# Attention group C: three pairs of score banks, one bank for transposed blocks and one for values

## The chip, the cores and the metric

One core of a Trainium2 chip runs the whole program. The metric is device time in microseconds (us). TensorE (PE) does the matmuls and the transposes, VectorE (DVE) and ScalarE (ACT) work on tiles, GpSimd (POOL) helps them, and SyncE (SP) issues the DMAs. PE writes to PSUM, a memory of 8 banks of 512 float32 per partition. Each engine executes its own list of instructions in order; a wait on a semaphore holds up everything behind it in that list.

## The reference, cut to what matters

The model has two layers. Each has three attention groups over 1024 positions, an output projection and a gated MLP. The change concerns group C, differential attention: four heads, each with two softmax maps over keys of width 32 and a distance bias; the second map is subtracted from the first with a learned weight, and the difference multiplies the values.

```python
logits = jnp.einsum('bqhid,bshid->bhiqs', qb, k).astype(f32) * scale
bias = -slopes[:, None, None, None] * jnp.abs(qp[:, None] - pos[None, :])[None, None]
p = jax.nn.softmax(logits + bias, axis=-1)
a = (p[:, :, 0] - lam * p[:, :, 1]).astype(v.dtype)
return jnp.einsum('bhqs,bshe->bqhe', a, v)
```

## The kernel before, in words

A layer's attention is a row of 32 units: units 0 to 7 are group B, units 8 to 15 group C (U_C is 8), units 16 to 31 group A (U_A is 16). A unit is one head and one half of the queries (512 of them, in four tiles of 128). Its work has these parts.

- Scores (`score_item`, L1645): one item is a tile of 128 queries against all 1024 keys, two PSUM banks wide. A unit of A or B has 4 items. A unit of C has 8, two maps for each query tile.
- Maximum (`max_item`, L1250 in group C, L1253 in the others): DVE adds the distance bias to the item in PSUM and takes its row extreme in one pass.
- Exponential (`exp_item`, L925): ACT reads the item from PSUM and writes it to SBUF, and sums the rows.
- Mix (`mix_maps`, group C alone): the second map, scaled by the ratio of the row sums, is added to the first. DVE does it for three query tiles (L1316, L1317, L1322), GpSimd for the first one (L708, L710), for which DVE only computes the ratio.
- Transposes and value product: in steps s = 0 to 7 PE transposes four 128x128 blocks of the probabilities into one PSUM bank (L1717), ACT copies the bank to SBUF (L987), and in groups A and B DVE computes a low part from it as well (L1358, called ptl). Three steps later (LAG) PE multiplies the copy with the values (L1679 in group C, L1683 and L1684 in A and B), which adds up over the eight steps in one bank.
- Spread reciprocals (L1730, called the norm): DVE inverts the row sums (`reciprocal_sums`, L1331), PE transposes them with a broadcast into a bank, ACT copies that bank to `nrm` (`copy_norm`, L961).
- Output sum (`sum_output`, L1340 in group C, L1343 in the others): DVE multiplies or adds the value bank. In A and B ACT copies one half of the bank first (`copy_part`, L970). Then ACT and GpSimd split the result into a high and a low part (L975, L700).

The units are staggered. While unit x is transposed, the items of the next unit are scored, reduced and exponentiated: items 2 to 7 at steps 0 to 5 of x (`STEP_OF[6]`). At steps 6 and 7 items 0 and 1 of the unit after the next follow (`EARLY_STEP_OF`). On ACT the exponentials of items 1 to 7 stand at steps 0 to 6 (`EXP_STEP_OF[6]`), and item 0 of the unit behind at step 7; in group C each stands ahead of the copy of its step. On DVE the mixes 0 to 3 of the next unit stand at steps 1, 4, 6 and 7, the last ahead of the maximum of item 1. PE begins step 0 of a C unit only when all four mixes are done. These orders are written out by hand in `pe_unit`, `act_unit` and `dve_unit`; no planner is at work.

The eight banks: two pairs for scores (banks 0 and 1, banks 2 and 3), taken in turn, so that a score waits for the exponential two items back; banks 4 and 5 for transposed blocks in turn, so that step s waits for the copy of s-2 (`transposed_free`); banks 6 and 7 for values, by the half of the queries. The norm is written to the value bank of the other half, at step 6, when the output sum of the unit before has read it, and ACT copies it out at step 6 or, in group C, 7. The output sum of the unit before stands at step 3 on DVE, behind the maximum of that step.

## Time and profile before

| what | us |
|---|---|
| median of 3 runs (lowest, highest) | 2998.17 (2997.57, 2999.02) |
| the profiled execution, its own time | 2998.82 |
| its span, first to last instruction | 2997.0 |
| PE busy | 2899.7 (97%) |
| DVE busy | 1991.8 (66%) |
| ACT busy | 1316.1 (44%) |
| POOL busy | 457.0 (15%) |
| mean granted TensorE clock | 0.993 of full speed |

The time of a run is a little longer than the span, as it holds what lies around the first and the last instruction. Busy shares are means over the whole program. Group C is transposed from 361 to about 499 us in layer 0, and from 1834 to about 1972 us in layer 1; its scores begin two units earlier.

### The profile page before, as it was taken

To read this page: it belongs to the slowest core of one execution; us is meant where nothing else is said; L and a number is where in the kernel's file an instruction comes from. 1 tells how busy PE (TensorE), PEld (TensorE's weight loads), DVE (VectorE), ACT (ScalarE), POOL (GpSimd) and SP (SyncE) were. 2 spreads that over 40 slices of the span, in tenths; PEclk is the share of its full clock that TensorE was granted. 3 is DMA by queue.
4 is the path that set the end of the run, shared out by engine and by line. 5 is a ranking of instruction groups with operands and counts; after the bars stand their busy time and mean duration, and the time that the engine had idled before them with its cause. 6 is when DMAs were issued, how large, how long until landed. Compare 5 with 4: busy or idle time off the path is not lost.

```text
span 2997.0 us, 36868 instructions
## 1 busy us (share of the span) xinstructions
PE 2899.7 (97%) x13564; PEld 2315.2 (77%) x13564; DVE 1991.8 (66%) x2312; ACT 1316.1 (44%) x1839; POOL 457.0 (15%) x243
## 2 busy tenths in 40 slices
PE   7999889999999999999999998899999999999998
PEld 5777656888788888888877785578887888888887
DVE  3987887982465556556678778889716565556555
ACT  4326888992322222222333287889714212212223
POOL 1211332223300000000131023322341000000002
PEclk9999999999999999999999999999999999999999
DMA  5455332432112111111135633234312111111102
GB/s 195 151 169 126 83 82 61 93 91 76 43 56 60 53 42 56 42 42 42 40 132 200 171 90 71 64 85 100 104 45 68 43 43 56 42 42 56 56 28 57
DMA packets 236372, 236.48 MB, mean 79 GB/s; under 512 B 59488, under 2 KB 199520, under 8 KB 236256
## 3 DMA queue, kind: packets, MB, share of 16 engines
q1 hardware_dynamic: 236256, 234.94, 27.8%
q8 instruction: 72, 1.18, 0.2%
q14 instruction: 44, 0.36, 0.0%
HBM read 184.04 MB, written 50.86 MB: 78 GB/s over the span
## 4 chain that ended last, share of the span: by engine, by line
PE 85%; DVE 7%; issue 4%; ACT 3%; DMA 1%; SPq 0%; POOL 0%; ACTq 0%; DVEq 0%
PE ps L1795 29%; PE ps L1810 16%; PE ps L1545 16%; PE ps L1645 8%; PE ps L1717 6%; PE ps L1683 3%; PE ps L1684 3%; DVE ps L1250 2%; PE ps L1679 2%; PE ps L1780 2%; PE ps L1576 1%; PE ps L1730 1%; DVE prob L1322 1%; DVE rstd L1395 0%; DVE r L1235 0%
## 5 line engine op out<-in xcount | busy, mean ns | idle before, releaser
L1645 PE MATMUL ps<-stack 128*128 128x512 f32 (+1 forms) x1152 | 347.5, 419 | 44.1 <-ACT prob L925 19.1
L1444 DVE TENSOR_TENSOR xT<-ps,xT 128x512 f32<-128x512 f32 x352 | 241.9, 691 | 214.4 <-PE ps L1810 214.2
L1645 PEld LDWEIGHTS ps<-stack 128*128 128x128 f32 (+1 forms) x1152 | 206.7, 191 | 154.9 <-ACT prob L925 51.3
L1717 PEld LDWEIGHTS ps<-cst,prob 128*128 128x128 f32 x2048 | 254.7, 142 | 89.1 <-issue 19.9
L1717 PE MATMUL ps<-cst,prob 128*128 128x128 f32 x2048 | 310.5, 275 | 7.5 <-issue 4.0
L925 ACT ACTIVATE prob<-ps,nmx 128x1024 f32<-128x1024 f32 x256 | 284.6, 1112 | 22.8 <-PE ps L1717 12.3
L1358 DVE TENSOR_TENSOR ptl<-ps,pth 128x512 fp32r<-128x512 f32 x384 | 259.3, 685 | 47.6 <-ACT pth L987 40.9
L1409 DVE SCALAR_TENSOR_TENSOR cv<-u,vec,cv 128x1024 f32<-128x1024 f32 x176 | 225.8, 1283 | 88.0 <-ACT cv L1064 77.8
L1076 ACT ACTIVATE ah<-cv 128x1024 fp32r<-128x1024 f32 x44 | 46.7, 1061 | 533.2 <-DVE cv L1422 533.2
L1795 PE MATMUL ps<-xgh,w0h 128*128 128x512 f32 x704 | 274.0, 389 | 2.6 <-ACT sq L1056 2.6
L1795 PE MATMUL ps<-xgl,w0h 128*128 128x512 f32 x704 | 273.9, 389 | 0.0
L1795 PE MATMUL ps<-xgh,w0l 128*128 128x512 f32 x704 | 273.9, 389 | 0.0
L1253 DVE TENSOR_REDUCE nmx<-ps 128x1 f32<-128x1024 f32 x192 | 234.0, 1219 | 60.0 <-PE ps L1645 58.5
L1064 ACT ACTIVATE cv<-u,vec 128x1024 f32<-128x1024 f32 x88 | 109.6, 1246 | 354.4 <-DVE u L1403 353.8
L987 ACT ACTIVATE pth<-ps 128x512 fp32r<-128x512 f32 x384 | 229.0, 597 | 68.8 <-PE ps L1717 59.9
L1795 PE MATMUL ps<-xgh,w1h 128*128 128x512 f32 x640 | 249.8, 390 | 4.1 <-DVE u L1403 4.1
L1795 PE MATMUL ps<-xgh,w1l 128*128 128x512 f32 x640 | 249.7, 390 | 0.0
L1795 PE MATMUL ps<-xgl,w1h 128*128 128x512 f32 x640 | 249.5, 390 | 0.0
L1810 PE MATMUL ps<-ah,dnh 128*128 128x512 f32 x640 | 249.1, 389 | 0.0
L1810 PE MATMUL ps<-ah,dnl 128*128 128x512 f32 x640 | 249.0, 389 | 0.0
L1810 PE MATMUL ps<-al,dnh 128*128 128x512 f32 x640 | 249.0, 389 | 0.0
L1403 DVE TENSOR_TENSOR u<-ps,rstd 128x512 f32<-128x512 f32 x176 | 118.7, 688 | 195.1 <-PE ps L1795 195.0
(239 smaller groups left out, 5554.4 us busy)
## 6 DMA issues: line engine op xcount, KB each, us to landing
wraw<-in_w_up SPq DMA_DIRECT2D x88, 512.0 KB, 4.7
draw<-in_w_down SPq DMA_DIRECT2D x22, 1024.0 KB, 4.9
stack<-ka_d SPq DMA_DIRECT2D x64, 256.0 KB, 5.7
wraw<-in_w_in SPq DMA_DIRECT2D x30, 512.0 KB, 4.2
vst<-v_d SPq DMA_DIRECT2D x48, 256.0 KB, 3.8
x_d<-xT SPq DMA_DIRECT2D x2, 4096.0 KB, 17.6
wraw<-in_w_out SPq DMA_DIRECT2D x16, 512.0 KB, 5.4
stack<-qc_d SPq DMA_DIRECT2D x64, 128.0 KB, 3.4
```

The costliest lines, as they stand in the source:

```text
L925: act.activation(two(dst), score_banks(i), ACT.Exp, bias=nmx[:, b, i:i + 1], scale=scale, accum_out=rsum[:, b, i:i + 1]).then_inc(exp_done, 1)
L987: act.activation((ptf if x["group"] == "C" else pth)[:, s % NPT, :], ps[:, 4 + s % 2, :], ACT.Copy).then_inc(pt_hi, 1)
L1253: dve.tensor_reduce(nmx[:, b, i:i + 1], src, AX.XY, ALU.max, negate=True).then_inc(max_done, 1)
L1358: dve.tensor_tensor(ptl[:, s % NPT, :], ps[:, 4 + s % 2, :], pth[:, s % NPT, :].bitcast(F32), ALU.subtract).then_inc(pt_lo, 1)
L1403: ins = dve.tensor_tensor(u[:, c, 1 + b * HALF:1 + (b + 1) * HALF], ps[:, base + 2 * c + b, :], rstd[:, b * HALF:(b + 1) * HALF], ALU.mult)
L1409: return dve.scalar_tensor_tensor(cv[:, c, :], u[:, c, k:k + T], vec[:, bass.ds(f + (V_CONV + 2 * k * FT + c * FT), 1)], cv[:, c, :], ALU. ...
L1444: ins = dve.tensor_tensor(xs, ps[:, 4 + j % 4, :], xs, ALU.add)
L1545: ins = pe.matmul(outs[b], a, x_[:, b * HALF:(b + 1) * HALF], start=start and n == 0, stop=stop and n == 2)
L1645: ins = pe.matmul(score_banks(i)[:, kh, :], st[q][0:rows, c0:c0 + P], st[k][0:rows, kh * HALF:(kh + 1) * HALF], start=n == 0, stop=n == le ...
L1717: ins = pe.transpose(ps[:, 4 + s % 2, m * P:(m + 1) * P], prob[:, b, m, s * P:(s + 1) * P], ident)
L1795: ins = pe.matmul(ps[:, base + 2 * c + b, :], a[:, o:o + P], x_[:, k, b * HALF:(b + 1) * HALF], start=k == 0 and n == 0, stop=k == KT - 1 ...
L1810: ins = pe.matmul(ps[:, 4 + j % 4, :], a[:, f, t * P:(t + 1) * P], x_[:, slot + f, b * HALF:(b + 1) * HALF], start=n == 0, stop=n == 5)
```

## The change: what it does

In group C the scores take three pairs of banks in turn (0 and 1, 2 and 3, 4 and 5), by the table `PAIRS`. The first C unit keeps the two pairs of before; the second uses the table mirrored. Bank 6 holds all transposed blocks of group C, bank 7 all its values. The spread reciprocals take pair 1 (bank 2) between its items 3 of one unit and 0 of another, in the last C unit bank 5; they move on PE from step 6 to step 3, and their copy on ACT from step 7 to step 4. The output sum of the unit before moves on DVE ahead of the maximum of step 3, and in the first C unit ACT's copy of a half moves ahead of the exponential of step 3.

The waits follow the banks. A score of the items 2 to 5 (and of item 1 from the fourth C unit on) waits for the exponential three items back; the others wait for two back. Item 0 also waits for the copy of the spread reciprocals two units back. Item 2 of the second C unit waits for the last low part of group B. In group C step s of the transposes waits for the copy of s-1, and the first value product waits for the output sum of the unit before. Groups A and B keep their banks. The first A unit gets two more waits, on copies of the spread reciprocals.

The diff, with lines of its context left out:

```diff
--- before.py
+++ after.py
@@ -351,9 +351,32 @@
-        def score_banks(i):
-
-            return ps[:, 2 * ((i + 1) % 2):2 * ((i + 1) % 2) + 2, :]
+        PAIRS = (1, 2, 0, 1, 2, 0, 2, 0)
+        NORM_PAIR = 1
+        def score_pair(x, i):
+            c = x["k"] - U_C
+            if x["group"] != "C" or c == 0:
+                return (i + 1) % 2
+            return (2 - PAIRS[i] if c == 1 else PAIRS[i])
+        def score_banks(x, i):
+            n = 2 * score_pair(x, i)
+            return ps[:, n:n + 2, :]
+        def trans_bank(x, s):
+            return ps[:, 6 if x["group"] == "C" else 4 + s % 2, :]
+        def value_bank(x):
+            return 7 if x["group"] == "C" else 6 + x["half"]
+        def norm_bank(x):
+            if x["group"] != "C":
+                return 7 - x["half"]
+            return 5 if x["k"] == U_A - 1 else 2 * NORM_PAIR
@@ -922,7 +945,7 @@
                         dst, scale = prob[:, b, i, :], 1.0
-                    act.activation(two(dst), score_banks(i), ACT.Exp, bias=nmx[:, b, i:i + 1],
+                    act.activation(two(dst), score_banks(x, i), ACT.Exp, bias=nmx[:, b, i:i + 1],
                                    scale=scale, accum_out=rsum[:, b, i:i + 1]).then_inc(exp_done, 1)
@@ -958,7 +981,7 @@
                     act.wait_ge(o_ready, l * NU + x["u"] + O_CREDIT)
-                    act.activation(nrm[:, :], ps[:, 7 - x["half"], :], ACT.Copy).then_inc(norm_copied, 1)
+                    act.activation(nrm[:, :], ps[:, norm_bank(x), :], ACT.Copy).then_inc(norm_copied, 1)
@@ -977,6 +1000,8 @@
                         second = nx and nx["group"] == "C"
+                        if s == 3 and x["k"] == U_C:
+                            copy_part(prev)
                         item = EXP_STEP_OF[own_items(nx)].get(s) if nx else None
@@ -984,14 +1009,14 @@
                         act.wait_ge(av_done, l * (8 * NU) + x["u"] * 8 + s + 1 - NPT + AV_CREDIT)
-                        act.activation((ptf if x["group"] == "C" else pth)[:, s % NPT, :], ps[:, 4 + s % 2, :], ACT.Copy).then_inc(pt_hi, 1)
+                        act.activation((ptf if x["group"] == "C" else pth)[:, s % NPT, :], trans_bank(x, s), ACT.Copy).then_inc(pt_hi, 1)
                         if not second and item is not None:
                             exp_item(nx, item)
-                        if s == 3 and prev:
+                        if s == 3 and prev and x["k"] != U_C:
                             copy_part(prev)
...
                             hi_mix(prev)
-                        if s == (7 if x["group"] == "C" else 6):
+                        if s == (4 if x["group"] == "C" else 6):
                             copy_norm(x)
@@ -1241,7 +1266,7 @@
                     dve.wait_ge(scores_done, l * NS + x["item0"] + i + 1)
-                    src = score_banks(i)
+                    src = score_banks(x, i)
                     if x["group"] == "C":
@@ -1337,7 +1362,7 @@
                         dve.wait_ge(mix_lo, l * NU + x["u"] + MIX_CREDIT)
-                        dve.tensor_tensor(osum[rows, :], ps[rows, 6 + x["half"], :], nrm[rows, :], ALU.mult).then_inc(o_ready, 1)
+                        dve.tensor_tensor(osum[rows, :], ps[rows, value_bank(x), :], nrm[rows, :], ALU.mult).then_inc(o_ready, 1)
                         return
@@ -1347,6 +1372,8 @@
                             mix_maps(nx, MIX_STEPS[s])
+                        if s == 3 and x["group"] == "C":
+                            sum_output(prev)
                         if nx and s in STEP_OF[own_items(nx)]:
@@ -1358,7 +1385,7 @@
                             reciprocal_sums(x)
-                        if s == 3 and prev:
+                        if s == 3 and prev and x["group"] != "C":
                             sum_output(prev)
@@ -1631,7 +1658,13 @@
                         pe.wait_ge(z_ready, l * NT + NT - 1 + i)
-                    pe.wait_ge(exp_done, l * NS + it - 1 + EXP_CREDIT)
+                    c = x["k"] - U_C if x["group"] == "C" else 0
+                    far = (c >= 1 and 2 <= i <= 5) or (c >= 2 and i == 1 and c > 2)
+                    pe.wait_ge(exp_done, l * NS + it - (2 if far else 1) + EXP_CREDIT)
+                    if i == 0 and (c >= 2 or x["k"] == U_A):
+                        pe.wait_ge(norm_copied, l * NU + x["u"] - 2 + 1 + N_CREDIT)
+                    if c == 1 and i == 2:
+                        pe.wait_ge(pt_lo, l * (8 * NAB) + U_C * 8 + PT_CREDIT)
                     qt = i // 2 if x["group"] == "C" else i
@@ -1642,7 +1675,7 @@
                         for kh in range(2):
-                            ins = pe.matmul(score_banks(i)[:, kh, :], st[q][0:rows, c0:c0 + P], st[k][0:rows, kh * HALF:(kh + 1) * HALF],
+                            ins = pe.matmul(score_banks(x, i)[:, kh, :], st[q][0:rows, c0:c0 + P], st[k][0:rows, kh * HALF:(kh + 1) * HALF],
                                             start=n == 0, stop=n == len(terms) - 1)
@@ -1659,6 +1692,13 @@
+                    if x["group"] == "C":
+                        if s == 0:
+                            pe.wait_ge(norm_copied, l * NU + x["u"] + N_CREDIT)
+                        pe.wait_ge(pt_hi, l * (8 * NU) + x["u"] * 8 + s)
+                        return
+                    if x["k"] == U_A and s == 1:
+                        pe.wait_ge(norm_copied, l * NU + x["u"] + N_CREDIT)
                     y, n = (x, s - 1) if s >= 2 else (prev, s + 7)
@@ -1675,8 +1715,12 @@
                     if x["group"] == "C":
+                        if s == 0 and x["k"] == U_C:
+                            pe.wait_ge(o_read, l * NAB + x["u"] + O_CREDIT)
+                        elif s == 0:
+                            pe.wait_ge(o_ready, l * NU + x["u"] + O_CREDIT)
                         pe.wait_ge(pt_hi, l * (8 * NU) + x["u"] * 8 + s + 1)
-                        pe.matmul(ps[:, 6 + b, :], vfull[x["par"]][:, s, :], ptf[:, s % NPT, :],
+                        pe.matmul(ps[:, value_bank(x), :], vfull[x["par"]][:, s, :], ptf[:, s % NPT, :],
                                   start=s == 0, stop=s == 7).then_inc(av_done, 1)
@@ -1714,20 +1758,23 @@
                         for m in range(4):
-                            ins = pe.transpose(ps[:, 4 + s % 2, m * P:(m + 1) * P], prob[:, b, m, s * P:(s + 1) * P], ident)
+                            ins = pe.transpose(trans_bank(x, s)[:, m * P:(m + 1) * P], prob[:, b, m, s * P:(s + 1) * P], ident)
                         ins.then_inc(trans_done, 1)
...
                             value_product(prev, 8 + s - LAG)
-                        if s == 6:
+                        if s == (3 if x["group"] == "C" else 6):
                             pe.wait_ge(dinv_done, l * NU + x["u"] + 1)
-                            if prev and prev["group"] == "C":
+                            if x["group"] == "C":
+                                if nx["group"] == "C":
+                                    pe.wait_ge(exp_done, l * NS + nx["item0"] + 4 + EXP_CREDIT)
+                            elif prev and prev["group"] == "C":
                                 pe.wait_ge(o_ready, l * NU + prev["u"] + 1 + O_CREDIT)
...
                             for m in range(4):
-                                ins = pe.transpose(ps[:, 7 - b, m * P:(m + 1) * P], dinv[:, m:m + 1].to_broadcast([P, P]), ident)
+                                ins = pe.transpose(ps[:, norm_bank(x), m * P:(m + 1) * P], dinv[:, m:m + 1].to_broadcast([P, P]), ident)
                             ins.then_inc(norm_done, 1)
...
```

## Rows read from the trace of the kernel before

**Rows 1.** The page, part 1: busy us of each engine over the span.

```profile
PE 2899.7 (97%) x13564; PEld 2315.2 (77%) x13564; DVE 1991.8 (66%) x2312; ACT 1316.1 (44%) x1839; POOL 457.0 (15%) x243
```

**Rows 2.** Windows, a unit each: length, PE, PEld, DVE, ACT, POOL; clock, DMA, GB/s.

```profile
393.96:411.34 17.38, 15.57 (x68) 9.07 (x68) 15.55 (x30) 14.43 (x27) 6.48 (x3) 1.00 0.25 69
411.34:429.12 17.78, 15.80 (x69) 9.07 (x69) 15.87 (x30) 14.44 (x27) 6.48 (x3) 1.00 0.37 82
```

**Rows 3.** Timeline of DVE, one round: start, duration, instruction; idle before and releaser.

```profile
392.53 1.26 DVE L1250 CUSTOM_DVE_ANT_0 ps<-ps,dtab 128x1024 f32<-128x1024 f32 x1
...
397.13 1.22 DVE L1250 CUSTOM_DVE_ANT_0 ps<-ps,dtab 128x1024 f32<-128x1024 f32 x1
...
400.62 1.23 DVE L1250 CUSTOM_DVE_ANT_0 ps<-ps,dtab 128x1024 f32<-128x1024 f32 x1 [1.03 <-PE ps L1645]
...
402.38 1.23 DVE L1250 CUSTOM_DVE_ANT_0 ps<-ps,dtab 128x1024 f32<-128x1024 f32 x1
...
404.15 1.23 DVE L1250 CUSTOM_DVE_ANT_0 ps<-ps,dtab 128x1024 f32<-128x1024 f32 x1 [0.47 <-PE ps L1645]
...
405.30 0.68 DVE L1340 TENSOR_TENSOR osum<-ps,nrm 64x512 f32<-64x512 f32 x1
...
405.91 1.23 DVE L1250 CUSTOM_DVE_ANT_0 ps<-ps,dtab 128x1024 f32<-128x1024 f32 x1
...
409.91 1.27 DVE L1250 CUSTOM_DVE_ANT_0 ps<-ps,dtab 128x1024 f32<-128x1024 f32 x1
```

**Rows 4.** Timeline of PE in the same round: scores, transposes, value products, norm.

```profile
397.31 0.63 PE L1717 MATMUL ps<-cst,prob 128*128 128x128 f32 x4
...
399.70 0.73 PE L1645 MATMUL ps<-stack 128*128 128x512 f32 x2 [0.90 <-ACT prob1a L925]
...
400.27 0.60 PE L1717 MATMUL ps<-cst,prob 128*128 128x128 f32 x4
...
400.71 1.02 PE L1679 MATMUL ps<-ptf,vfull 128*128 128x512 f32 x2
...
401.29 0.91 PE L1645 MATMUL ps<-stack 128*128 128x512 f32 x2
...
402.03 0.60 PE L1717 MATMUL ps<-cst,prob 128*128 128x128 f32 x4
...
402.47 1.02 PE L1679 MATMUL ps<-ptf,vfull 128*128 128x512 f32 x2
...
410.42 0.60 PE L1730 MATMUL ps<-cst,dinv 128*128 128x128 f32 x4
```

**Rows 5.** Timeline of ACT in the same round: exponential of item 1, copy of step 0.

```profile
398.44 1.11 ACT L925 ACTIVATE prob1a<-ps,nmx 128x1024 f32<-128x1024 f32 x1 [0.54 <-DVE nmx L1250]
...
399.55 0.59 ACT L987 ACTIVATE ptf<-ps 128x512 f32<-128x512 f32 x1
```

**Rows 6.** Timeline of PE in unit 14, packed around the norm.

```profile
479.33 1.02 PE L1679 MATMUL ps<-ptf,vfull 128*128 128x512 f32 x2
480.19 0.60 PE L1730 MATMUL ps<-cst,dinv 128*128 128x128 f32 x4
480.55 1.18 PE L1645 MATMUL ps<-stack 128*128 128x512 f32 x4
481.57 0.60 PE L1717 MATMUL ps<-cst,prob 128*128 128x128 f32 x4
```

**Rows 7.** Timeline of DVE in units 7 and 8: ptl, maximum, output sum, a mix.

```profile
362.19 0.69 DVE L1358 TENSOR_TENSOR ptl<-ps,pth 128x512 fp32r<-128x512 f32 x1
...
362.80 1.22 DVE L1250 CUSTOM_DVE_ANT_0 ps<-ps,dtab 128x1024 f32<-128x1024 f32 x1
...
369.97 0.68 DVE L1343 TENSOR_TENSOR osum<-ps,osum 64x512 f32<-64x512 f32 x1 [0.61 <-ACT osum L970]
...
372.31 1.78 DVE L1322 SCALAR_TENSOR_TENSOR prob<-prob1a,rinv,prob 128x1024 f32<-128x1024 f32 x1
```

**Rows 8.** Window of 2 us in layer 1, unit 8, columns as in rows 2.

```profile
1838.00:1840.00 2.00, 2.00 (x7) 1.61 (x6) 1.59 (x5) 1.88 (x4) 0.25 (x1) 0.50 0.02 4
```

## The prediction

> **What bounds the kernel now.** I read the busy shares first: TensorE is busy for 97% of the span [rows 1], so most of the kernel is matmul-bound and an edit of group C can't touch it. Next I read busy time unit by unit. The change concerns group C alone, units 8 to 15 of each layer. In a C unit of 17.4 us the reader is to see PE at 15.57, DVE at 15.55 and ACT at 14.43 [rows 2]: none is full, so the unit is bound by a chain that goes round the engines. To find it I read three engines' instructions of one unit in order of time [rows 3 to 5].
>
> I call the score items of the unit after next a0 to a7, the first item behind them b0, and T(s), V(s) the transposes and the value product of step s. One round is from max a0 (DVE, 392.53) to max b0 (409.91), 17.38 us. DVE idles in it twice: 1.03 us ahead of max a3 (400.62) and 0.47 ahead of max a5 (404.15) [rows 3]. Before max a3 the chain is: the last mix, max a1 (397.13), exp a1 on ACT (398.44), and only then the score of a3 on PE (399.70, after 0.90 idle), since with two pairs a3 takes the pair that exp a1 empties [rows 3 to 5]. From there PE runs packed: a step is 1.76 (T at 400.27 and 402.03), of which T to V is 0.44, V to the next score 0.75, score to T 0.57; V to the next T is 1.32 [rows 4]. From max a6 (405.91) to max b0 DVE is packed for 4.00 us [rows 3]. N, the spread reciprocals at step 6 (410.42), stands where PE next waits for an exp anyway [rows 4], so N is free now.
>
> **Part 1, the third pair.** The scores of items 2 to 5 (and 1 from the fourth unit on) wait for an exp one further back. So score a3 can follow as soon as T(0) and V(5) are through: 397.31 + 0.44 + 0.75 = 398.50, its end at 399.24, and max a3 0.19 later (DVE follows a matmul's end by that: 399.70 + 0.73 to 400.62), 399.43 instead of 400.62 [rows 3, 4]. Taken alone this gives DVE 1.19 us.
>
> **Part 2, one transposed bank.** T(s) now waits for the copy of s-1, where it waited for s-2. In ACT's queue copy(0) stands behind exp a1, and exp a1 stands behind max a1 and DVE's mixes: copy(0) starts at 399.55 and takes 0.59, so 400.14 [rows 5]. T(1) can start at about 400.19; before it started at 400.27 [rows 4]. The score of a4 stands behind T(1) and V(6) in PE's queue. So the lead of 1.19 us ends at T(1): a4 is scored only 0.08 sooner than before, and DVE idles before a4 instead of before a3. That is what is late next.
>
> In the other steps this wait is met: beside T (0.60) ACT has an exp of 1.11, then the copy of 0.59, a ring of 1.70 against PE's own 1.76 [rows 4, 5]. The Trainium skill (Perfetto Trace Analysis, "Optimizing Tensor Performance", Matmuls) says that groups of matmuls should rotate through different PSUM banks, so that the evacuation of one overlaps the next. By that rule each of the eight transposes of a unit would pay for the single bank; the rows say that only T(1) does.
>
> **Part 3, one value bank.** V(0) of a unit now waits for the output sum of the unit before, moved on DVE ahead of max a5. V(7) of that unit starts at 402.39 (402.47 less 0.08) and ends 1.02 later, DVE follows by 0.19, the sum takes 0.68, and PE follows by about 0.1 (an estimate between 0.05 and that 0.19): 404.38 [rows 3, 4]. By PE's own pace V(0) would be at 402.39 + 1.32 + 0.44 = 404.15. Cost 0.23; bounds 0.05 (every wake-up at its shortest) and 0.68 (the whole sum exposed). I take 0.23, which is built from the nearest rows.
>
> **Part 4, N moved from step 6 to step 3.** The four transposes are the same; they stand now between V(0) and the score of a6, in the packed stretch. Where PE is packed around N, V to N is 0.86, N to the score 0.36, N to the next T 1.38 with a score of four matmuls [rows 6]; two fewer end 0.45 sooner (1.18 against 0.73). So V to T grows from 1.32 to 0.86 + 0.93 = 1.79: cost 0.47. Bounds: 0 (if it all fits under what PE waits for) and 0.86. N's wait for exp a3 is met, as T(3) has waited for copy(2), which is behind it in ACT's queue. What N leaves at step 6 gains nothing: the score there waits for exp a7, which DVE sets. Copying N out at step 4 on ACT, 0.6 us, lies in the time in which ACT waits for max a6.
>
> **The new round.** V(0) 404.38, N 405.24, score a6 ends 0.36 + 0.73 later at 406.33, max a6 at 406.52 instead of 405.91. Before, DVE itself set this point, with the sum (405.30) behind a5; moving the sum gives DVE a slack that it can't use. Then DVE's 4.00 us, b0 at 410.52. The round is 17.99, +0.61. The longer rounds of 17.78 [rows 2] pay their 0.4 more around the same sum, where it now overlaps in part: I take +0.3. Of the rounds of units 9 to 13 three are short and two long in each layer: 3 x 0.61 + 2 x 0.3 = 2.4. Unit 14 passes the same points up to its last mix: +0.6. From unit 15 on PE has no gap between its pieces (how they close up around N: [rows 6]); N only changes its place: 0.
>
> **The first C unit.** Score 2 of unit 9 takes banks 4 and 5, and so waits for the last ptl of unit 7, which starts on DVE at 362.19: end 362.88, score at 362.98, max 2 at 363.90 [rows 7]. Before, that max started right behind the ptl, at 362.80. +1.1. Later in the unit V(0) waits for ACT's copy of a half and DVE's sum (ends 370.65 before); with the same steps max 6 comes 1.6 later, of which DVE's slack gives 0.5 back. I take +1.1, between 0.7 and 1.6. PE stands for some 4 us ahead of that score. In layer 1 a stretch of this unit already shows a granted clock of 0.50 of full speed, 1.2 GHz, after several shorter stands [rows 8]; if layer 0 falls too, that is 1 us more.
>
> **Sum.** 2.4 + 0.6 + 1.1 = 4.1 a layer, 8.2 in two. The profiled execution took 2998.82 (span 2997.0), 0.65 above the median of 2998.17: from its own time the new one is 3007.0, on the median 3006.4. Forecast 3006.4, its own range 3003.5 to 3010. About 0.2%, 6 us, is what can be told from no change.
>
> **Rivals.** (A) The other side: T(1) isn't held. If copy(0) ends before 399.07, where T(1) could go behind the early score (398.50 + 0.57), the 1.19 us come through to a4; V(0)'s wait and N take 0.7 back, and the round is 16.9. That is -0.5 for three rounds and unit 14, -0.87 for two, +1.1: -2.6 a layer, 2992.9. If N and the sum were hidden as well, DVE would lose its 1.50 of idle in six stretches: 2981. Against it: exp a1 stands behind DVE's packed mixes, and copy(0) behind exp a1, a full microsecond late for it. (B) N and the sum's wait are hidden (bounds 0 and 0.05), and only the first unit costs: +2.2, 3000.4. For it: TensorE's weight loads overlap, and my rows on N come from a stretch with other scores. (C) Worse: the sum now runs beside GpSimd's mix and is stretched to its upper bound, 0.45 more in six stretches of each layer, and layer 0's clock falls: +6.4, 3012.8. For it: one mix on DVE grew from 1.28 to 1.78 while GpSimd worked [rows 7]; against it: that was another operation. (D) The pair isn't used as it says, since items 6, 7 and 0 keep the near wait: the same time as the forecast, as T(1) takes over either way.
>
> **Chances.** Forecast 0.58 (with D), A 0.13, B 0.17, C 0.12. Slower by over 0.2% (above 3004.2): 0.91 of the forecast and all of C, 0.65. Within 0.2%: the rest of the forecast, B and half of A, 0.28. Faster: the other half of A, 0.07. The range leaves out A and a little above C: 2999 to 3013.
>
> **What would show it.** Right: in a middle C unit the score of a3 comes 1.2 us sooner, while T(1) starts right behind copy(0); DVE idles ahead of max a4 and ahead of max a6, over 1 us each; PE waits some 0.2 before V(0); N is followed by its score at once; the round is near 18.0; max 2 of unit 9 comes 1.1 later. Wrong: rounds of 17.3 or less; or equal rounds, with N in a stall; or a loss outside group C.

## The result and the profile after

| | before | after |
|---|---|---|
| median of 6 runs, us (lowest, highest) | 2998.06 (2996.99, 2999.02) | 3009.72 (3006.04, 3012.50) |
| the profiled execution, us | 2998.82 | 3008.77 |
| its span, us | 2997.0 | 3007.0 |

The ratio of the times is 1.0036, 95% interval 1.0026 to 1.0046: the change makes the kernel slower, by 11.7 us on the medians and by 10.0 in the profiled pair. Forecast was 3006.4, with 2999 to 3013 as the range.

The busy shares don't tell the story. The page, part 1 of after, beside [rows 1]:

```profile
PE 2896.9 (96%) x13564; PEld 2317.5 (77%) x13564; DVE 1990.2 (66%) x2312; ACT 1315.5 (44%) x1839; POOL 457.1 (15%) x243
```

Each engine does the same work in more time, so the loss is waiting. Part 5 of the page groups it by line; the last column is idle time ahead of the group and the releaser of most of it. Before, scores and transposes:

```profile
L1645 PE MATMUL ps<-stack 128*128 128x512 f32 (+1 forms) x1152 | 347.5, 419 | 44.1 <-ACT prob L925 19.1
...
L1717 PE MATMUL ps<-cst,prob 128*128 128x128 f32 x2048 | 310.5, 275 | 7.5 <-issue 4.0
```

After, the same two lines of the code:

```profile
L1678 PE MATMUL ps<-stack 128*128 128x512 f32 (+1 forms) x1152 | 369.1, 438 | 27.3 <-ACT prob L948 12.8
...
L1761 PE MATMUL ps<-cst,prob 128*128 128x128 f32 x2048 | 312.7, 276 | 35.0 <-ACT ptf L1012 20.7
```

The idle time ahead of scores falls by 16.8 us: the part that waits for exponentials, over all three of their tiles, goes from 43.3 to 17.9, and 9.3 are new, for the last ptl of group B. Ahead of the transposes 27.5 us are added, and 20.7 of what stands there now waits for the copy out of the one bank. The wait has changed its line and grown.

Where in time: I measured every round of group C, from the maximum of one unit's item 0 to that of the next, in both profiled executions.

| round, by the unit that is transposed | before, layer 0 / 1 | after, layer 0 / 1 | change | predicted |
|---|---|---|---|---|
| unit 8 | 19.25 / 19.74 | 22.32 / 22.31 | +3.07 / +2.57 | +1.1 |
| units 9 to 13, sum | 87.68 / 87.69 | 90.40 / 90.41 | +2.72 / +2.72 | +2.4 |
| unit 14, to the maximum of item 7 | 16.22 / 16.25 | 16.97 / 16.96 | +0.75 / +0.71 | +0.6 |

Together that is +12.5 us, where 8.2 was predicted. The span grew by 10.0, so in this pair 2.5 us came back outside group C. The single times of before in the experiments below lie between 2992 and 3003, so a difference of that size needs no cause in the change. The stretches outside group C, where the code is nearly the same in every kernel of this document, say so too: together they took between 2741.9 and 2754.3 us in the twelve profiled executions, 2750.2 in before's and 2747.6 in after's.

**A middle unit.** Windows of after, beside [rows 2]: length, PE, PEld, DVE, ACT, POOL, clock, DMA share, GB/s:

```profile
398.22:416.33 18.11, 15.39 (x68) 9.25 (x68) 15.44 (x30) 14.38 (x27) 6.48 (x3) 1.00 0.23 66
416.33:434.47 18.14, 15.40 (x68) 9.26 (x68) 15.69 (x30) 14.35 (x27) 6.47 (x3) 1.00 0.37 80
```

Timeline of DVE in the round from max a0 to max b0, beside [rows 3]:

```profile
396.79 1.26 DVE L1275 CUSTOM_DVE_ANT_0 ps<-ps,dtab 128x1024 f32<-128x1024 f32 x1
...
401.39 1.23 DVE L1275 CUSTOM_DVE_ANT_0 ps<-ps,dtab 128x1024 f32<-128x1024 f32 x1
...
403.72 1.26 DVE L1275 CUSTOM_DVE_ANT_0 ps<-ps,dtab 128x1024 f32<-128x1024 f32 x1
...
406.62 1.23 DVE L1275 CUSTOM_DVE_ANT_0 ps<-ps,dtab 128x1024 f32<-128x1024 f32 x1 [1.16 <-PE ps L1678]
...
407.77 0.68 DVE L1365 TENSOR_TENSOR osum<-ps,nrm 64x512 f32<-64x512 f32 x1
408.38 1.23 DVE L1275 CUSTOM_DVE_ANT_0 ps<-ps,dtab 128x1024 f32<-128x1024 f32 x1
...
410.90 1.23 DVE L1275 CUSTOM_DVE_ANT_0 ps<-ps,dtab 128x1024 f32<-128x1024 f32 x1 [1.23 <-PE ps L1678]
...
414.90 1.27 DVE L1275 CUSTOM_DVE_ANT_0 ps<-ps,dtab 128x1024 f32<-128x1024 f32 x1
```

Take each start from the round's own beginning. Max a3 comes at 6.93, where before it came at 8.09: the third pair delivers its 1.16. Max a4 comes at 9.83, before at 9.85: the whole lead is gone one item later, as idle time of 1.16. Max a6 comes at 14.11 where it was at 13.38, with 1.23 of idle ahead of it.

PE in the same round, beside [rows 4], shows who took it:

```profile
398.71 0.66 PE L1761 MATMUL ps<-cst,prob 128*128 128x128 f32 x4 [0.83 <-ACT ptf L1012]
...
401.57 0.63 PE L1761 MATMUL ps<-cst,prob 128*128 128x128 f32 x4 [0.88 <-DVE prob L1347]
...
402.50 1.03 PE L1678 MATMUL ps<-stack 128*128 128x512 f32 x2
404.45 0.66 PE L1761 MATMUL ps<-cst,prob 128*128 128x128 f32 x4 [0.93 <-ACT ptf L1012]
...
405.41 1.02 PE L1678 MATMUL ps<-stack 128*128 128x512 f32 x2
406.27 0.60 PE L1761 MATMUL ps<-cst,prob 128*128 128x128 f32 x4
...
408.03 0.60 PE L1761 MATMUL ps<-cst,prob 128*128 128x128 f32 x4
408.70 1.10 PE L1723 MATMUL ps<-ptf,vfull 128*128 128x512 f32 x2
409.64 0.60 PE L1777 MATMUL ps<-cst,dinv 128*128 128x128 f32 x4
410.00 0.71 PE L1678 MATMUL ps<-stack 128*128 128x512 f32 x2
```

The score of a3 (402.50) no longer idles. T(1), 404.45, waits 0.93 for the copy of step 0. V(0), 408.70, starts 0.67 behind T(3) where V follows T by 0.44 elsewhere, which I read as its wait for the output sum; two rounds on, the trace names it at the same place:

```profile
445.14 1.10 PE L1723 MATMUL ps<-ptf,vfull 128*128 128x512 f32 x2 [0.27 <-DVE osum L1365]
```

N, 409.64, stands 0.94 behind V(0) in the packed stretch. The first line, 398.71, is T(7) of the unit before. It too waits for the copy of the step before it, which stands behind an exponential. That costs nothing: T(7) comes 1.92 into the round and came 2.00 into it before, and T(0), held by the last mix, comes at 4.78 in both. So of the waits for that copy on the page about half, those ahead of T(7), are idle time without a loss.

ACT, beside [rows 5], shows why the copy of step 0 is late; the first exponential is that of item a1:

```profile
402.71 1.11 ACT L948 ACTIVATE prob1a<-ps,nmx 128x1024 f32<-128x1024 f32 x1 [1.04 <-DVE nmx L1275]
...
403.81 0.59 ACT L1012 ACTIVATE ptf<-ps 128x512 f32<-128x512 f32 x1
404.29 1.11 ACT L948 ACTIVATE prob<-ps,nmx 128x1024 f32<-128x1024 f32 x1
```

T(0) is done at 402.20, but ACT, in order, first waits for max a1 (1.04 of idle) and does exp a1. The copy could have started while ACT idled.

**The first unit.** PE and then DVE of after while unit 8 is transposed, beside [rows 7]:

```profile
363.68 1.19 PE L1678 MATMUL ps<-stack 128*128 128x512 f32 x2 [4.66 <-DVE ptl L1385]
364.67 1.05 PE L1761 MATMUL ps<-cst,prob 128*128 128x128 f32 x4
...
372.24 1.10 PE L1723 MATMUL ps<-ptf,vfull 128*128 128x512 f32 x2 [0.89 <-DVE osum L1368]
...
377.98 0.71 PE L1678 MATMUL ps<-stack 128*128 128x512 f32 x2 [0.69 <-ACT prob L948]
```

```profile
365.06 1.23 DVE L1275 CUSTOM_DVE_ANT_0 ps<-ps,dtab 128x1024 f32<-128x1024 f32 x1 [1.53 <-PE ps L1678]
...
374.42 1.23 DVE L1275 CUSTOM_DVE_ANT_0 ps<-ps,dtab 128x1024 f32<-128x1024 f32 x1 [1.20 <-PE ps L1678]
```

The score of item 2 stands 4.66 us until the last ptl has read its banks, as predicted. Behind it matmuls take longer: this score 1.19 instead of 0.73, the transposes 1.05 instead of 0.60. Windows of the two layers (the clock is the third number from the end), beside [rows 8]:

```profile
361.00:365.00 4.00, 1.32 (x4) 1.05 (x5) 2.53 (x4) 1.20 (x2) 1.78 (x1) 0.55 0.00 0
365.00:369.00 4.00, 4.00 (x16) 3.26 (x15) 2.62 (x6) 2.45 (x5) 0.00 (x0) 0.60 0.00 0
```

```profile
1840.00:1844.00 4.00, 2.27 (x8) 1.91 (x9) 2.47 (x4) 1.40 (x3) 0.96 (x1) 0.50 0.00 0
1844.00:1848.00 4.00, 4.00 (x19) 3.24 (x18) 2.62 (x8) 3.22 (x5) 0.51 (x1) 0.72 0.01 2
```

The granted clock falls to 0.50 of full speed, 1.2 GHz, in both layers. Before it fell in layer 1 alone. Measured from each round's start in layer 0, max 2 comes 1.61 later than before, max 4 2.50, max 5 3.19, max 6 3.20 and the next round 3.07. ACT gives a last piece:

```profile
376.19 0.60 ACT L984 ACTIVATE nrm<-ps 128x512 f32<-128x512 f32 x1 [0.88 <-POOL osum L717]
```

The copy of N, moved to step 4, waits here for GpSimd, and the exponential of item 6 stands behind it.

### The profile page after: what moved, and what is told of

It reads as the page before. It is cut to its first block, busy times and chain, and to the rows that moved or that the text cites. A ratio compares the mean times of both kernels' runs of the same rounds, so it can differ in the third digit from the quotient of the medians.

```text
span 3007.0 us, 36900 instructions
## 1 busy us (share of the span) xinstructions
PE 2896.9 (96%) x13564; PEld 2317.5 (77%) x13564; DVE 1990.2 (66%) x2312; ACT 1315.5 (44%) x1839; POOL 457.1 (15%) x243
## 4 chain that ended last, share of the span: by engine, by line
PE 85%; DVE 7%; issue 3%; ACT 3%; DMA 1%; POOL 1%; SPq 0%; ACTq 0%; DVEq 0%; POOLq 0%
PE ps L1842 29%; PE ps L1857 16%; PE ps L1572 16%; PE ps L1678 8%; PE ps L1761 6%; PE ps L1727 3%; PE ps L1728 3%; DVE ps L1275 2%; PE ps L1723 2%; PE ps L1827 2%; PE ps L1603 1%; PE ps L1777 1%; DVE rstd L1422 0%; DVE r L1260 0%; DVE prob L1347 0%
## 5 line engine op out<-in xcount | busy, mean ns | idle before, releaser
L1678 PE MATMUL ps<-stack 128*128 128x512 f32 (+1 forms) x1152 | 369.1, 438 | 27.3 <-ACT prob L948 12.8
L1761 PE MATMUL ps<-cst,prob 128*128 128x128 f32 x2048 | 312.7, 276 | 35.0 <-ACT ptf L1012 20.7
L1678 PEld LDWEIGHTS ps<-stack 128*128 128x128 f32 (+1 forms) x1152 | 213.3, 192 | 122.7 <-issue 56.1
L948 ACT ACTIVATE prob<-ps,nmx 128x1024 f32<-128x1024 f32 x256 | 284.8, 1112 | 23.5 <-PE ps L1761 12.1
```

Of the source, the lines that this page charges most:

```text
L948: act.activation(two(dst), score_banks(x, i), ACT.Exp, bias=nmx[:, b, i:i + 1], scale=scale, accum_out=rsum[:, b, i:i + 1]).then_inc(exp_d ...
L1678: ins = pe.matmul(score_banks(x, i)[:, kh, :], st[q][0:rows, c0:c0 + P], st[k][0:rows, kh * HALF:(kh + 1) * HALF], start=n == 0, stop=n == ...
L1761: ins = pe.transpose(trans_bank(x, s)[:, m * P:(m + 1) * P], prob[:, b, m, s * P:(s + 1) * P], ident)
```

## The experiments

Rounds are named by the unit that is transposed; each ratio is against runs of the kernel before on the same chip.

**1. The first unit.** Unit 9's items get pairs that leave banks 4 and 5 alone until item 4:

```diff
-            return (2 - PAIRS[i] if c == 1 else PAIRS[i])
+            return ((1, 0, 1, 0, 2, 0, 2, 0)[i] if c == 1 else PAIRS[i])
...
-                    far = (c >= 1 and 2 <= i <= 5) or (c >= 2 and i == 1 and c > 2)
+                    far = (c == 1 and i == 4) or (c >= 2 and 2 <= i <= 5) or (c >= 2 and i == 1 and c > 2)
...
-                    if c == 1 and i == 2:
+                    if c == 1 and i == 4:
```

> The kernel after, but unit 9's items use the pairs 1, 0, 1, 0, 2, 0, 2, 0, so that banks 4 and 5 come in only at item 4 and the wait for group B's last low part stands there. Theory (the first C unit's loss is the score of item 2 held behind the last ptl, and TensorE's clock that falls in the stand of 4.66 us it makes): the stand goes, the round of unit 8 goes from 22.3 to about 19.3 (before: 19.25 in layer 0, 19.74 in layer 1) plus up to 0.9 for the first value product's wait; 2.0 to 3.0 us less a layer, 4 to 6 us less than the 3009.7 of the kernel after: 3005. Rival (the loss there comes from the first value product's wait for the output sum of unit 7): the stand goes, but the round stays above 21 and the time within 1.5 us of 3009.7.

Measured: 3006.51 us, ratio 1.0032 (1.0020 to 1.0044). The round of unit 8 is 19.89 in layer 0 and 20.53 in layer 1, so 2.4 and 1.8 shorter than after's; units 9 to 13 stay at 17.91 to 18.29. In layer 0 the clock stays at 1.00, in layer 1 it still falls to 0.50 (1844 to 1848 us). The wait for the last ptl, with the clock that falls in it, makes up most of the first unit's loss. V(0)'s wait of 0.86 remains. The reading rests on the rounds: the ratio alone can't be told from that of the changed kernel, 1.0036.

**2. The lead is lost to ACT's order.** In group C the copy of step 0 goes ahead of exp a1:

```diff
-                        if second and item is not None:
+                        first = second and not (s == 0 and x["group"] == "C")
+                        if first and item is not None:
                             exp_item(nx, item)
...
-                        if not second and item is not None:
+                        if not first and item is not None:
                             exp_item(nx, item)
```

> The kernel after, with ACT's copy of step 0 of a C unit ahead of the exponential of item 1. Theory (the third pair's lead is lost at the transposes of step 1, which wait for copy 0 behind that exponential): the transposes of step 1 start about 1.1 us sooner, max a4 about 1.1 sooner; the transposes of step 2 then wait for copy 1 behind exp a2 and keep 0.6 of it, so the round goes from 18.11 to about 17.5, 6 rounds a layer: 7 us less than the kernel after, 3002.5. Rival (a step of PE sets the round, not that copy): rounds and time unchanged, 3009.7.

Measured: 3000.28 us, ratio 1.0009 (1.0000 to 1.0018): 3.6 us above before on the same chip, where the changed kernel was 11.7 above in its own comparison. The rounds of units 9 to 13 are 17.44, 17.54, 17.39, 17.61 and 17.45. PE, then ACT, in the round that starts at 392.92:

```profile
397.70 0.63 PE L1762 MATMUL ps<-cst,prob 128*128 128x128 f32 x4 [0.88 <-DVE prob L1348]
...
399.49 0.60 PE L1762 MATMUL ps<-cst,prob 128*128 128x128 f32 x4
...
401.76 0.66 PE L1762 MATMUL ps<-cst,prob 128*128 128x128 f32 x4 [0.35 <-ACT ptf L1013]
```

```profile
398.37 0.60 ACT L1013 ACTIVATE ptf<-ps 128x512 f32<-128x512 f32 x1 [0.57 <-PE ps L1762]
398.86 1.11 ACT L948 ACTIVATE prob1a<-ps,nmx 128x1024 f32<-128x1024 f32 x1
```

T(1) follows T(0) by 1.79 and waits for nothing; after it was 2.88. Part of the gain moves on to T(2), which now waits 0.35 for the copy of step 1. So the lead that the third pair gives was held at T(1) by the single bank together with ACT's order.

**3. N one step later.** N on PE at step 4, its copy at step 5:

```diff
-                        if s == (3 if x["group"] == "C" else 6):
+                        if s == (4 if x["group"] == "C" else 6):
...
-                        if s == (4 if x["group"] == "C" else 6):
+                        if s == (5 if x["group"] == "C" else 6):
                             copy_norm(x)
```

> The kernel after, with the spread reciprocals at step 4 on PE and their copy at step 5 on ACT, in group C. Theory (at step 3 they cost 0.47 a round, as they stand between the value product and the score of a6, which DVE waits for; at step 4 they stand behind that score and DVE has slack): max a6 0.5 sooner, round about 17.64, 12 rounds: 5.6 us less, 3004.1. Rival (they are hidden at step 3 too, and the value product's wait for the output sum is all of the loss): time unchanged within 1 us, 3009.7.

Measured: 3006.19 us, ratio 1.0036 (1.0022 to 1.0049); rounds 18.07 to 18.43, none shorter. DVE, PE and ACT of the round that starts at 394.07, in three views:

```profile
407.70 1.23 DVE L1275 CUSTOM_DVE_ANT_0 ps<-ps,dtab 128x1024 f32<-128x1024 f32 x1 [0.79 <-PE ps L1678]
...
412.31 1.23 DVE L1275 CUSTOM_DVE_ANT_0 ps<-ps,dtab 128x1024 f32<-128x1024 f32 x1 [0.46 <-PE ps L1678]
```

```profile
411.42 0.70 PE L1678 MATMUL ps<-stack 128*128 128x512 f32 x2 [0.41 <-ACT nrm L984]
```

```profile
410.68 0.59 ACT L984 ACTIVATE nrm<-ps 128x512 f32<-128x512 f32 x1
```

The shorter rounds that were expected, 17.64, did not come. Max a6 comes at 13.63 instead of 14.11: the 0.48 that N costs at step 3 is there. But the score of b0 needs N's bank, and N's copy at step 5 now stands behind exp a6 and the copy of the step, so b0 idles 0.46. The gain turned into a new wait, and an order of ACT is again what does it. Unit 14, where no such score follows, keeps the gain: 16.49 to the maximum of item 7, where after has 16.97.

**4. Is the third pair used at all?** Every score waits for the exponential two items back, nothing else changes:

```diff
-                    far = (c >= 1 and 2 <= i <= 5) or (c >= 2 and i == 1 and c > 2)
+                    far = False
```

> The kernel after, with every score waiting for the exponential two items back, as with two pairs: the third pair's room is not used. Theory (the third pair brings nothing in this kernel, since the transposes of step 1 start behind copy 0 either way): score a3 1.2 us later, max a4 and the round unchanged at 18.1, time within 1.5 us of 3009.7. Rival (the pair gives a part of its 1.19 us a round, and the other edits lose more than they seem to): rounds of 18.6 to 19.3, 6 to 14 us slower than the kernel after, 3016 to 3024.

Measured: 3007.02 us, ratio 1.0040 (1.0026 to 1.0054); rounds 17.94, 18.12, 18.17, 18.32 and 17.98, where after has 17.91, 18.11, 18.14, 18.29 and 17.95. In the changed kernel the third pair's early score is worth 0.03 us a round.

**5. The moves alone.** The kernel before with two pairs, its old banks, and the moves of N, of N's copy, of the output sum and of the half's copy:

```diff
-                        if s == (7 if x["group"] == "C" else 6):
+                        if s == (4 if x["group"] == "C" else 6):
                             copy_norm(x)
...
-                        if s == 6:
+                        if s == (3 if x["group"] == "C" else 6):
...
```

> The kernel before with its banks (two pairs, two transposed, two value banks), and only the moves of the change in group C: spread reciprocals at step 3, their copy at step 4, the output sum ahead of the maximum of step 3. Theory (the reciprocals cost 0.47 in the packed stretch of PE; the value product's wait for the sum, 0.23, isn't there with two value banks): max a6 about 0.4 later, the short rounds 17.4 go to 17.8, the long ones of 17.77 to 17.8 or 17.9; 1.8 us a layer, 3.7 in all: 1.0012 of the kernel before. Rival (the moves cost nothing and the banks all): rounds as before, 17.38 and 17.77, ratio 1.000. Rival (the moves are all of the loss in the steady rounds): 18.1, ratio 1.002 or more.

Measured: 3000.34 us, ratio 1.0011 (1.0003 to 1.0020). The rounds are 17.78, 17.82, 17.82, 17.82 and 17.82, sum 89.06 against 87.68 before: +1.4 a layer. V(0) waits for nothing here, as it has the other value bank. So of the +0.73 of unit 10's round 0.44 come with the moves, and 0.29 from what only the new banks add. N's place is the likely part of the moves, as its 0.48 in experiment 3 says, but the moves were not run one by one. Over group C of both layers the moves alone add 5.0 of the 12.5 us in this profile: the rounds of units 8 and 14 are longer too (19.92 and 20.42, and 16.68).

**6. Is the copy's order a gain by itself?** The kernel before with only experiment 2's edit:

> The kernel before, with ACT's copy of step 0 of a C unit ahead of the exponential of item 1: the order of e2_copy_first without the change's banks. Theory (with two pairs the score of a3 waits for that exponential anyway, so the order is worth something only with the third pair): rounds 17.38 and 17.77 within 0.1, ratio 1.000. Rival (the order is what gains, the pair nothing): rounds 0.6 shorter, 7 us less, ratio 0.9977.

Measured: 2999.93 us, ratio 1.0007 (0.9999 to 1.0016); rounds 17.64, 17.40, 17.80, 18.02 and 17.63, sum 88.49, 0.8 longer than before. PE in the round that starts at 392.10:

```profile
399.29 0.73 PE L1646 MATMUL ps<-stack 128*128 128x512 f32 x2 [0.92 <-ACT prob1a L925]
399.86 0.60 PE L1718 MATMUL ps<-cst,prob 128*128 128x128 f32 x4
```

With two pairs the score of a3 still waits for exp a1, and an earlier copy finds nobody who waits for it. The gain of experiment 2 needs the third pair. In unit 9's round the copy delays exp a1: it starts 6.18 into the round instead of 5.90, the score of a3 follows at 7.43 instead of 7.16, and the round is longer by that 0.27. In unit 10's round before, ACT had 0.54 of idle ahead of exp a1 [rows 5], and the round stays. Units 12 and 13, longer by about 0.25 too, were not traced.

**7. Both mended.** Experiment 1 with the copies of steps 0, 1 and 2 ahead of the exponentials (the line takes the place of the one in experiment 2):

```diff
+                        first = second and not (s < 3 and x["group"] == "C")
```

> The kernel after, with unit 9's items as in e1_first_unit and ACT's copies of steps 0, 1 and 2 of a C unit ahead of the exponentials of items 1, 2 and 3. Theory (after e2_copy_first the next thing held is the transposes of step 2, 0.35 behind copy 1 behind exp a2): PE is packed from the transposes of step 0 to the first value product, max a6 0.5 sooner than in e2, rounds near 17.0, round of unit 8 19.9; a layer's stretch from max a0 of unit 8 to max a7 of unit 15 near 140.5 us, where it is 142.6 before: 4 us less than before, ratio 0.9986. Rival (exponentials that come later hold scores a6, a7 or DVE's mixes instead): rounds stay at 17.5, ratio 1.0000 to 1.0010.

Measured: 2994.29 us, ratio 0.9990 (0.9981 to 0.9998). Rounds 16.79, 16.96, 16.99, 17.14 and 16.80; unit 8 20.14 in layer 0, without a fall of the clock, and 21.96 in layer 1 with one. The rounds are those that were expected.

**8. N out of the packed stretch as well.** Experiment 7 with N at step 4, its copy at step 5 ahead of the exponential, and item 0 on the far wait, that for the exponential three items back:

```diff
+                        if s == 5 and x["group"] == "C":
+                            copy_norm(x)
                         if first and item is not None:
                             exp_item(nx, item)
```

> e7_first_copies, with the spread reciprocals at step 4, their copy on ACT ahead of the exponential of step 5, and item 0 waiting for the exponential three items back. Theory (in e3_norm_step4 the 0.48 that max a6 gained was lost again, as the score of b0 waited for the copy of the reciprocals behind exp a6 and copy 5): with that copy ahead the gain stays, rounds near 16.5, the stretch of a layer near 137.5, ratio 0.9965, faster than the kernel before. Rival (the copy now delays exp a6 and with it score b0 or mix 2 by what it gains): rounds of 17.0 as e7, ratio 0.9986.

Measured: 2989.27 us, ratio 0.9979 (0.9970 to 0.9987): faster than both kernels, by 6.9 us than before on the same chip. Rounds 16.75, 16.73, 16.72, 16.74 and 16.72. Scores, T(1) and max a6 in the round that starts at 389.73:

```profile
395.43 1.02 PE L1681 MATMUL ps<-stack 128*128 128x512 f32 x2
396.29 0.60 PE L1764 MATMUL ps<-cst,prob 128*128 128x128 f32 x4
...
401.53 0.74 PE L1681 MATMUL ps<-stack 128*128 128x512 f32 x2
```

```profile
402.45 1.23 DVE L1278 CUSTOM_DVE_ANT_0 ps<-ps,dtab 128x1024 f32<-128x1024 f32 x1 [1.00 <-PE ps L1681]
```

T(1) is 0.86 behind the score of a3 and waits for nothing. The score of a6 (401.53) starts 1.04 behind V(0) (400.49), though N is no longer between them (it is at 403.40); it has the near wait, two items back, for exp a4, which ends 0.15 ahead of it. That leaves DVE 1.00 of idle, and is probably where the rounds stay 0.2 above the expected 16.5; a run with that wait moved was not made.

**9. What the third pair is worth once it counts.** Experiment 8 with items 1 to 5 on the near wait:

```diff
-                    far = (c == 1 and i == 4) or (c >= 2 and (i == 0 or 2 <= i <= 5)) or (c >= 2 and i == 1 and c > 2)
+                    far = c >= 2 and i == 0
```

> e8_norm4_too with the scores of items 1 to 5 waiting for the exponential two items back, as with two pairs; item 0 keeps its wait three items back. Theory (the third pair is worth its 1.19 us a round once the copies stand ahead of the exponentials): score a3 waits for exp a1 again, the transposes of step 1 start 1.2 later, max a6 about 1.0 later, rounds 17.7 instead of 16.73, 10 to 12 us more than e8_norm4_too: ratio to the kernel before 1.001 to 1.002. Rival (the order on ACT and the place of the reciprocals are all of the gain, the pair is worth nothing here either, as in e4_near_waits): rounds 16.7 to 16.9, ratio 0.998.

Measured: 3031.41 us, ratio 1.0105 (1.0086 to 1.0123); rounds 19.92, 19.79, 19.78, 19.91 and 19.90. The sign is as the theory has it, the size is a miss. PE, then ACT:

```profile
403.18 0.73 PE L1681 MATMUL ps<-stack 128*128 128x512 f32 x2 [0.92 <-ACT prob1a L948]
403.75 0.60 PE L1764 MATMUL ps<-cst,prob 128*128 128x128 f32 x4
...
406.13 0.74 PE L1681 MATMUL ps<-stack 128*128 128x512 f32 x2 [0.92 <-ACT prob L948]
```

```profile
404.38 0.60 ACT L1015 ACTIVATE ptf<-ps 128x512 f32<-128x512 f32 x1 [1.26 <-PE ps L1764]
404.88 1.11 ACT L948 ACTIVATE prob<-ps,nmx 128x1024 f32<-128x1024 f32 x1
```

I had counted one wait a round. The rows show a ring: score (403.18), T behind it (403.75), its copy (404.38), the exponential behind the copy (404.88), and the next score (406.13), 2.95 a step for the steps whose copy goes first. A third pair breaks that ring, and is worth 3.1 a round there, and 0.03 in the changed kernel. The 3.1 is measured against an order that suits two pairs badly. Against the kernel before, whose rounds of units 9 to 13 are 17.54 on average, experiment 8 gains 0.8 a round. What that order would do with two score pairs and two banks for transposed blocks was not run, so how much of the 0.8 is the pair's stays open.

**10. The changed kernel again**, unchanged, on another chip:

> The kernel after, unchanged, on the chip of the other run of this call, to have it beside e9. Theory: rounds of 17.9 to 18.3 as in its first profile, round of unit 8 between 21.5 and 22.3 by how long TensorE's clock stays down after the stand of 4.66 us; ratio 1.0036 to 1.0042, as six steady rounds and the first unit add 12.6 us in the two layers. Rival (the 2.7 us by which the first profile came out shorter than its rounds is real and lies outside group C): ratio 1.003 or less.

Measured: 3007.01 us, ratio 1.0027 (1.0015 to 1.0038). Its rounds are those of the first profile within 0.02: 17.93, 18.10, 18.13, 18.30 and 17.95, unit 8 22.01 and 22.13. The loss in group C repeats, 12.1 us against the first profile of before. The ratio stands for 8.3, below what the theory expected and in line with its rival's bound. But the rival, a real gain outside group C, isn't shown either: those stretches took 2745.7 us here and 2750.2 in before's profile, both inside the 2741.9 to 2754.3 of the twelve profiled executions. The interval reaches 11.4, and single runs of either kernel spread by 7 to 10 us.

## Why the prediction was right, and where it was off

The forecast of 3006.4 is 3.3 below the first median of after and 0.6 below the second. The direction and the mechanism held; by its own steps:

- Part 1 held: max a3 came 1.16 sooner, 1.19 was the number.
- Part 2 held. T(1) was put right behind copy(0), at 7.66 from the round's start, and stands at 404.45 - 396.79 = 7.66. Max a4 is 0.02 sooner, 0.08 was the number. Experiments 2 and 4 show that this is where the pair's gain goes: without the pair nothing changes, and with the copy first 0.57 of a round come back. Rival A (T(1) not held) is out by the trace itself (and its 2981 does not come out of its terms: 1.50 in six stretches, less the first unit's 1.1, gives 2982.4), and experiments 7 and 8 show it as what the change could have been, 16.7 to 17.1 a round, where the rival's sum had 16.9.
- The rule weighed there, to rotate matmul groups through PSUM banks (the Trainium skill, Perfetto Trace Analysis, "Optimizing Tensor Performance", Matmuls): of the eight transposes of a middle unit two show a wait for the single bank, T(1) 0.93 and T(7) 0.83, where the prediction had T(1) alone, and only T(1)'s costs time. Here the measurement decides: the queue in front of the copy set the price more than the number of banks.
- Part 3 held: V(0) is 0.67 behind T(3), so 0.23 late, the very term. That it fits to the hundredth is luck: the sum starts 0.05 behind V(7)'s end (407.77 against 407.72) and not 0.19, and PE follows the sum's end (408.45) by 0.25 and not 0.1. No run takes this wait away by itself. Rival B (N and sum hidden) is out.
- Part 4 held: V to N is 0.94, N to the score 0.36, and experiment 3 gives N's cost at max a6 as 0.48, where 0.47 was the term. That moving N frees nothing at its old place is seen too: in experiment 5 the moves only cost.
- The new round: 17.99 predicted, 18.11 measured. Max a6 at 14.11 was put at 13.99. V to N, 0.94 instead of 0.86, and T(2), 1.82 behind T(1) instead of 1.76, hold most of the difference. The rounds of units 9 to 13 together came to 2.7 for 2.4, and unit 14 to 0.75 for 0.6.
- **The failed step is the size of "The first C unit".** The wait was named right, with its place (score 2 at 362.98 in before's time; after's round runs 0.65 later, and 363.68 was found). Its price was not: +3.07 and +2.57 for +1.1. First, the clock: the text had it as one microsecond more if layer 0 fell too, and left it out of the sum. It fell in both layers, and longer than before in layer 1. In layer 0 max 4 comes 2.50 later, 1.4 more than the stand's 1.1 (362.98 and its maximum at 363.90, for 362.80), and I put that 1.4 down to the slow stretch. Experiment 1 bears this out: without the stand, its layer 1 with the fall and its layer 0 without one are 1.43 apart at max 4 (11.70 and 10.27 into the round), of which 0.64 is left at the round's end. In experiment 10, where the stretch is about half as long, max 4 is 2.01 late. Another 0.7 comes at max 5 behind V(0)'s wait, where 0.5 was counted; it comes without stand and fall too, as 0.78 in layer 0 of experiment 1. Second, DVE's slack was to give 0.5 back, and gave 0.13 (3.20 to 3.07), since N's copy waits for GpSimd ahead of exp 6 (the 0.88 above). In experiment 2, where that wait is 0.45, 0.58 comes back.
- Sum: 8.2 predicted, 12.5 in group C, 10.0 in the profiled span. That the time came nearer than the terms is luck: the stretches outside group C were 2.5 us shorter in this pair, which is inside their spread. Rival C's 3012.8 is as near to 3009.7 as the forecast, by half of its cause: the sum on DVE isn't stretched while GpSimd works (0.68 at 407.77, with GpSimd's part of the mix from 405.57 to 408.42), the clock did fall.
- Rival D (the pair not used as it says) is not the case: the score of a3 starts at once. It would have given the same time, as experiment 4 shows.

## What to carry to other kernels

A buffer more helps only as far as the next wait in the same queue. Before adding one, follow the early instruction to the next on its engine, ask what that one waits for, and in which order the engine that serves it works. Here the change cost 12 us in group C as built. With unit 9's pairs changed (experiment 1), three copies and N's ahead of the exponentials, N one step later and a far wait for item 0, the same eight banks made the kernel 0.2% faster.

An edit of order and one of buffers can each be worth nothing and pay together: the pair's early score alone 0.03 us a round (experiment 4), one copy moved alone a slight loss (6), both 0.57 a round better than the changed kernel (2). Price them as a pair. And where a stand of some microseconds is added ahead of packed matmuls, put the clock's fall into the sum, not beside it.

## What the hardware showed beyond that

- The stand of 4.66 us on PE goes with a half clock in both layers and in both profiles of the changed kernel, each time with a stretch of another length (361 to 369 us in the first, 359 to 364 in the second). In experiment 1, with stands of 0.90, 1.25 and 1.29 in layer 0 and 0.87, 0.90 and 1.26 in layer 1, it fell in layer 1 and not in layer 0; in experiment 6, with up to 1.46, in neither. A kernel whose clock falls in layer 1 alone gives the price of a fall for unit 8's round: 19.89 and 20.53 in experiment 1, 19.92 and 20.42 in 5, 20.14 and 21.96 in 7, 19.70 and 21.50 in 8, and 21.10 and 24.67 in 9, where the clock stays down about twice as long (1849 to 1863 us). So it costs 0.5 to 3.6 us. The Trainium skill (TensorE: Matmul & The Clock Gate, "What's actually happening") says that the throttled state is the default and that activity releases it; the trace agrees, with 0.50 behind the stand and 1.00 again while PE is packed.
- DVE follows a matmul's end by 0.19 us (score 410.00 for 0.71, max a6 410.90), but ACT starts 0.03 behind one (experiment 9: T at 403.75 for 0.60, copy at 404.38). The ends are modelled, and the output sum, on DVE as well, starts only 0.05 behind V(7)'s (407.77), so these gaps can't be read as the engines' own.
